# A block's first and last product open and close its sum, and each step puts the products ahead of the query projection

## The reference

```python
def block(xb):
    q = (xb @ w_q).reshape(PEER_BLOCK, PEER_HEADS, 2, PEER_KEY_DIM // 2)
    s1 = jnp.einsum('thd,nd->thn', q[:, :, 0], keys1)
    s2 = jnp.einsum('thd,nd->thn', q[:, :, 1], keys2)
    ...
    gate = jax.nn.softmax(sc, axis=-1)
    act = jax.nn.gelu(jnp.einsum('thkd,td->thk', u_tab[e], xb), approximate=False)
    return jnp.einsum('thk,thkd->td', gate * act, v_tab[e])
```

## Time and profile before

| | before |
|---|---|
| median of 3 runs | 2748.71 us (2748.07 to 2752.73) |
| the profiled execution | 2741.37 us |
| its span in the trace | 2739.6 us |
| PE busy | 2421.6 us (88%) |
| DVE busy | 1590.1 us (58%) |
| ACT busy | 900.0 us (33%) |
| moved by the DMA engines | 935.29 MB, 341 GB/s over the span |
| share of the gathers' queue | 60.8% of 16 engines' span |

### The profile page before, as it was taken

One profiled execution on the slowest core, in us unless ns is written; L12 is line 12 of the kernel. 1 busy time (PEld: TensorE's weight loads), 2 busy tenths in 40 slices (PEclk: granted clock), 3 DMA queues, 4 the chain that ended last, 5 costly groups with the idle time before them and its releaser, 6 DMA issues.

```text
span 2739.6 us, 26850 instructions
## 1 busy us (share of the span) xinstructions
PE 2421.6 (88%) x8530; PEld 1356.4 (50%) x8530; DVE 1590.1 (58%) x3736; ACT 900.0 (33%) x2386; POOL 793.3 (29%) x705
## 2 busy tenths in 40 slices
PE   6999999888998788799898898998998998888786
PEld 3555554356887544455444464443554444334332
DVE  2330012212487775798656798657788557666674
ACT  3100121021122332555424554334644324343332
POOL 0111100000133122343333334334343335444442
PEclk9999999999999889999999999999999999999999
DMA  6222316875898789999999999999999999999996
GB/s 261 100 100 100 115 51 231 328 310 193 314 344 340 280 339 426 406 411 381 426 427 425 425 371 409 426 427 426 413 369 424 423 426 417 427 416 426 426 420 277
DMA packets 143568, 935.29 MB, mean 341 GB/s; under 512 B 16914, under 2 KB 28434, under 8 KB 41026
## 3 DMA queue, kind: packets, MB, share of 16 engines
q0 software_dynamic: 96928, 687.39, 60.8%
q1 hardware_dynamic: 33842, 204.77, 19.1%
q10 hardware_dynamic: 12656, 41.42, 3.8%
HBM read 898.33 MB, written 35.19 MB: 341 GB/s over the span
## 4 chain that ended last, share of the span: by engine, by line
PE 32%; DMA 26%; DVE 12%; ACT 3%; DVEq 2%; issue 2%; POOL 1%; ACTq 1%; POOLq 0%
DMA ring<-in_peer_uv,e_idx 24%; PE e_acc L1803 14%; PE e_acc L1732 5%; DVE ring L1936 5%; PE e_qs L1821 3%; PE e_B L1714 3%; PE e_A L1714 2%; DVEq L1938 2%; DMA e_wb<-in_w_out 1%; POOL ring L1536 1%; ACT e_diag L1652 1%; DMA e_mg<-in_w_late 1%; DVE e_f L1952 1%; PE e_A L948 1%; ACT e_coef L1645 1%
## 5 line engine op out<-in xcount | busy, mean ns | idle before, releaser
L1803 PE MATMUL e_acc<-ring,e_diag 128*128 128x512 f32 x2368 | 1114.8, 618 | 204.7 <-ACT e_diag L1652 204.5
L1536 POOL DMA_INDIRECT ring<-in_peer_uv,e_idx x640 | 753.0, 1177 | 1398.3 <-PE e_acc L1803 1008.8
L1936 DVE CUSTOM_DVE_ANT_0 ring<-ring,e_xb 128x1024 f32<-128x1024 f32 x640 | 774.8, 1224 | 418.9 <-DMA ring<-in_peer_uv,e_idx 397.9
L1803 PEld LDWEIGHTS e_acc<-ring,e_diag 128*128 128x128 f32 x2368 | 448.2, 196 | 785.6 <-issue 481.6
L1642 ACT ACTIVATE e_act<-e_dots 128x2 f32<-128x2 f32 x320 | 65.1, 203 | 734.3 <-DVEq L1938 731.3
L534 PE MATMUL pj<-held,ring 128*128 128x512 f32 x512 | 225.2, 593 | 0.0
L1652 ACT ACTIVATE e_diag<-ident,e_coef 128x128 f32<-128x128 f32 x592 | 206.1, 394 | 20.9
L568 PE MATMUL pj<-ring,held 128*128 128x512 f32 x352 | 156.4, 599 | 10.1 <-DMA ring<-in_w_big 7.9
L1645 ACT ACTIVATE e_coef<-e_act,e_gate 128x1 f32<-128x1 f32 x640 | 153.9, 287 | 23.1 <-issue 1.1
L534 PEld LDWEIGHTS pj<-held,ring 128*128 128x128 f32 x512 | 94.8, 190 | 107.3 <-issue 107.3
L1821 PEld LDWEIGHTS e_qs<-e_h2T,e_w_head 128*128 128x128 f32 x1200 | 141.1, 195 | 10.0 <-issue 9.7
(11 more groups left out here) (405 smaller groups left out, 2338.8 us busy)
## 6 DMA issues: line engine op xcount, KB each, us to landing
e_wb<-in_w_out SPq DMA_DIRECT2D x49, 1024.0 KB, 9.4
ring<-in_w_big SPq DMA_DIRECT2D x18, 2048.0 KB, 9.0
e_w_head<-in_w_q ACTq DMA_DIRECT2D x30, 1024.0 KB, 9.1
ring<-in_w_mod SPq DMA_DIRECT2D x8, 2048.0 KB, 10.3
ring<-in_peer_uv,e_idx POOLq DMA_INDIRECT x640, 12.3
wm<-in_w_mod SPq DMA_DIRECT2D x4, 2048.0 KB, 18.2
e_m<-scratch_mod_rows SPq DMA_DIRECT2D x15, 512.0 KB, 14.7
e_m<-scratch_xbcT SPq DMA_DIRECT2D x7, 1024.0 KB, 14.6
```

What stands on the lines that cost most here:

```text
L1536: nc.gpsimd.indirect_dma_start(expert[:, u % RING, :], None, dr["peer_uv"], bass.IndirectOffsetOnAxis(idx[:, h % 4, s:s + 1], 0)).then_inc ...
L1803: mm = nc.tensor.matmul(acc[:, c * 512:(c + 1) * 512], diag[:, v % RING, :], expert[:, v % RING, D + c * 512:D + (c + 1) * 512], start=Fal ...
L1936: nc.vector.tensor_tensor_reduce(expert[:, u % RING, 0:D], expert[:, u % RING, 0:D], xb[p % 2][:, :], 1.0, 0.0, ALU.mult, ALU.add, dots[:, ...
```

## The change

Three edits. The first product of a block opens the accumulation and the last one closes it, so the 4 matmuls of zeros per block are gone, with the tile of zeros. Who waited for `f_mm` waits for the last product's `slot_free`. And in `body` of PE, `begin` (now only a wait) and `products` stand ahead of the query projection (n = 0) and of the scores (n = 2).

```diff
+FIRST_PRODUCT = [min(u for u in range(SLOTS * p, SLOTS * (p + 1)) if not ON_VECTOR[u]) for p in range(BLOCKS)]
+LAST_PRODUCT = [max(u for u in range(SLOTS * p, SLOTS * (p + 1)) if not ON_VECTOR[u]) for p in range(BLOCKS)]
...
             def block_sum(p):
                 if p:
-                    act.wait_ge(f_mm, p + 1)
+                    act.wait_ge(slot_free, earlier(LAST_PRODUCT[p]) + 1)
...
                     pe.wait_ge(late_free, LATE_UNITS)
-                for c in range(2):
-                    nc.tensor.matmul(acc[:, c * 512:(c + 1) * 512], zero[:, :], z512, start=True, stop=False)
-
-            def end(p):
-                for c in range(2):
-                    last = nc.tensor.matmul(acc[:, c * 512:(c + 1) * 512], zero[:, :], z512, start=False, stop=True)
-                last.then_inc(f_mm, 1)
...
                         mm = nc.tensor.matmul(acc[:, c * 512:(c + 1) * 512], diag[:, v % RING, :],
-                                              expert[:, v % RING, D + c * 512:D + (c + 1) * 512], start=False, stop=False)
+                                              expert[:, v % RING, D + c * 512:D + (c + 1) * 512],
+                                              start=v in FIRST_PRODUCT, stop=v in LAST_PRODUCT)
                     mm.then_inc(slot_free, 1)
...
             def body(m, n):
                 c = m + 2
+                if m >= 0:
+                    if n == 0 and (m == FIRST_ON_PE or m and m % HP == 0):
+                        begin(m // HP)
+                    products(m, n)
                 if c < HEADS:
...
-                if m >= 0:
-                    if n == 0 and (m == FIRST_ON_PE or m and m % HP == 0):
-                        begin(m // HP)
-                    products(m, n)
-                    if m % HP == HP - 1 and n == GROUPS - 1:
-                        end(m // HP)
...
             def first_sum():
-                dve.wait_ge(f_mm, 1)
+                dve.wait_ge(slot_free, earlier(LAST_PRODUCT[0]) + 1)
```

More of the change, by code:

```diff
@@ L1284, in experts @@
         dots, act_v, coef = sb("dots", [P, 2, TOPK]), sb("act", [P, 2]), sb("coef", [P, 4, 2])
-        diag, zero = sb("diag", [P, RING, P]), sb("zero", [P, P])
+        diag, ready = sb("diag", [P, RING, P]), sb("ready", [P, 1])
         ss, root, rr = sb("ss", [P, 1]), sb("root", [P, 1]), sb("rr", [P, 1])
@@ L1322, in experts @@
         dots_ready, diag_ready = sem("dots_ready"), sem("diag_ready")
-        f_mm, acc_free, ss_ready, ms_ready, root_ready, y_ready, y_out, row_in = (
-            sem("f_mm"), sem("acc_free"), sem("ss_ready"), sem("ms_ready"), sem("root_ready"), sem("y_ready"), sem("y_out"),
+        acc_free, ss_ready, ms_ready, root_ready, y_ready, y_out, row_in = (
+            sem("acc_free"), sem("ss_ready"), sem("ms_ready"), sem("root_ready"), sem("y_ready"), sem("y_out"),
             sem("row_in"))
@@ L1696, in _ @@
             ident = t["ident"]
-            z512 = zero[:, :].unsqueeze(1).to_broadcast([P, 4, P])
             def product(p, i):
@@ L2064, in _ @@
             dve_back_init()
-            nc.vector.memset(zero[:, :], 0.0).then_inc(const_ready, 1)
+            nc.vector.memset(ready[:, :], 0.0).then_inc(const_ready, 1)
             interleave(late, back, scan, merge, prepare, body, finish, body_first=True)
```

## The result

| | before | changed kernel |
|---|---|---|
| median, timed side by side (4 runs each) | 2748.79 us (2748.07 to 2752.73) | 2794.37 us (2788.72 to 2798.81) |
| ratio, 95% interval | | 1.0162 [1.0145, 1.0180] |
| span of the profiled execution | 2739.6 us | 2792.8 us |
| PE busy | 2421.6 us | 2444.1 us |
| moved by the DMA engines | 935.29 MB, 341 GB/s | 935.29 MB, 335 GB/s |

The changed kernel is 1.6% slower, some 45 us. The forecast was 2749.8 us with a range up to 2760 us, so it was wrong, and wrong by far more than any of its terms. PE has 40 matmul rows fewer (8490 for 8530) and yet is busy 22.5 us longer.

The account below looks back on a forecast made before the run. The prediction took gathers on the DMA engines as the bound. Its terms, -1.7 - 1.7 + 4.5 = +1.1 us, put the profiled 2741.37 us at 2742.5 and the median 2748.71 at 2749.8 us, range 2741 to 2760 us.

Parts of the forecast that it names:

- What bounds the kernel now: Experts' part: gathers keep DMA full while PE has time to spare; 17.6 us of holes at ends of blocks 0 to 2.
- All other heads: PE's two waits in heads away from the holes: caught up within the head, cost nothing; 2.1 + 3.4 us per head at stake.
- The order at the end of a block: PE's changed list around head 16: 29.5 us to the products of (16, 3), 27.4 before; (16, 0) 7.0 us earlier.
- E: End of PE's products of head 15, step 7, where the 29.5 us sum starts; expected about 1.7 us later.
- its fifth term: Two experts' products on PE (products 1) behind the 2.1 us wait for ACT, at 3.44 us.
- What this does to the gathers: Refill after (16, 3) 1.2 us late per place; taken as 1.5 at three places, 4.5 us, bounds 0 and 10.5.
- the head before: Head 15, also full of scan: waits behind its projection and scores make its end about 1.7 us later.
- rival 1: Waits at three block ends cool PE and hold DVE up: 2755.8 us, up to 2763; chance 0.28.
- The zeros: Pairs of 1.72 us on PE: 1.7 us gained at the end, 1.7 at the first pair; block ends counted elsewhere.
- Rival 2: Holes at block ends close as slots of (16, 0) come free 7 us earlier: 2731 us, half 2740; chance 0.17.
- The signs that were named: Block ends: POOL's first wait 7 us shorter, PE idle 2 and 3.4 us, DVE's L1964 waiting 3 us at three places.
- The two signs that were to prove the prediction wrong: Three places' missing DMA time over 5 us from 17.6 us, or a plain stretch, as at 2580, below 1.0.

Follow-up runs that it names:

- scan_heads_old: The changed kernel with PE's old order of projection, scores and products in heads m % 8 = 6, 7, 0, 1, beside the scan; 2740.97 us, ratio 0.9972.
- first_zeros_gone: The kernel before without the pair of zero matmuls ahead of each block's first product; 2741.13 us, ratio 0.9978.
- last_zeros_gone: The kernel before without the pair of zero matmuls behind each block's last product; 2739.63 us, ratio 0.9975.
- S_copy_behind: The changed kernel with only ACT's copy of S moved behind the run of its step; 2760.51 us, ratio 1.0047.
- zeros_only: The kernel before with all zero matmuls gone and PE's order of projection, scores and products kept; 2737.14 us, ratio 0.9962.
- order_only: The kernel before, zeros kept, with products moved ahead of the projection and the scores on PE; 2809.13 us, ratio 1.0224.
- projection_moved: The changed kernel with products ahead of the projection only, scores ahead of products as before, no zeros; 2758.08 us, ratio 1.0047.

## Why the prediction was wrong, by its own steps

**What bounds the kernel now.** The reading holds: the gathers bound the kernel, and an edit can cost time only by making the DMA engines idle. What failed is the step after it, that the search for such places ended with the windows that already showed a hole. A full window doesn't say how much more PE could take. In head 14 both were full at once: DMA 1.01 and PE 42.75 of 45.4 us. The prediction had such a row in hand, three of its windows showed PE busy for all 20 us, and read from it only where the holes were.

**"All other heads" is the step that failed.** It priced the waits in all heads but the ones at the holes at nothing, since "PE is idle for a fifth of the time" in a plain stretch and "catches up within the head". For the 20 heads m % 8 in 2 to 5 that was nearly true: scan_heads_old has the waits there and is 7.2 us faster than before, and in the changed kernel the heads outside of the scan stretches lose 1.3 us. Of these 20 heads only 5, 13 and 21, right ahead of scan heads, lose something in the changed kernel, by the dot products 1.9, 3.9 and 5.3 us. For the scan heads ahead of a block's last one it was false: heads 6, 14 and 22 lose 21.1 us, in windows that had been full. The price stood in the text as what would be at stake if the cover were gone, "2.1 + 3.4 us per head"; measured in head 14 are waits of 1.99 and 3.29 us and 3.5 us of lower clock, of which 7.1 us came through. The idle share of one stretch at 2580 us had been used for all stretches.

**The order at the end of a block: the walk held, its price did not.** From E to the start of the products of (16, 3) the walk gave 29.5 us; the timeline of the changed kernel, from the row that follows (15, 7), has 1684.81 - 1653.39 = 31.42:

```profile
1653.39 1.04 PE L928 MATMUL e_A<-ident,held 128*128 128x128 f32 x8
...
1667.00 5.40 PE L1799 MATMUL e_acc<-ring,e_diag 128*128 128x512 f32 x8 [1.99 <-ACT e_diag L1656]
...
1684.81 3.61 PE L1799 MATMUL e_acc<-ring,e_diag 128*128 128x512 f32 x4 [3.29 <-ACT e_diag L1656]
```

The 1.9 us over the walk are the products at 1667.00, which took 5.40 us instead of the 3.44 of its fifth term. Both waits came out as worked out, 1.99 for 2.1 and 3.29 for 3.4. What this does to the gathers was taken as 1.5 us per place, 4.5 us. The intervals around the three ends cost 6.3, 5.7 and 5.1 us, 17.1 in all, nearly four times that and more than the upper bound of 10.5 us.

The starts of the products say which part failed. They lag by 28.7 us at (14, 7), 30.4 at (15, 7), 23.3 at (16, 0), 29.0 at (16, 1), 30.4 at (16, 2), 34.3 at (16, 3) and still 34.2 at (17, 7). So the head before did cost its 1.7 us, and (16, 0) did come 7.1 us earlier, as worked out (7.0). (16, 3) comes 5.6 us later than by the lag at (14, 7), for the 3.8 us of the prediction; the 1.9 us between them are the half clock of (16, 1), which the walk left to rival 1. Then the prediction took off most of the delay, since "before, this refill queued", and was left with 1.2 us. Nothing came off: a head later the lag is the same.

**The zeros.** -3.4 us was too small; -9.7 us is measured. The pair at the end was right: in the changed kernel the copy of the sum (L1631) starts at 2781.22, 3.74 us behind the start of the last products at 2777.48. The mis-sized part is the pairs at the ends of blocks 0 to 2, which had been put into the walk and vanished there in a sum with the other sign; by themselves they stand where PE has little time to spare, and first_zeros_gone and last_zeros_gone, 6.3 and 7.8 us faster, fit their being paid in full.

**The rivals.** Rival 1 had the right sign and part of the right mechanism: waits for ACT's diagonals, products at half clock behind them, and DVE's choice later (its wait for the copy of `S` is 63.7 us in 20 places, 18.0 in 4 before), though S_copy_behind has nearly the same waits of DVE, 57.9 us in 19 places, and loses 13 us where the changed kernel loses 46. It too looked only at three places, so its far end was 2763 us, and of the two it put the clock first: in head 14 the waits make 4.9 us of the 8.4 and the clock 3.5. The Trainium skill, "TensorE: Matmul & The Clock Gate", Part 1, says that an idle stretch returns the array to 1.2 GHz. The rows at 1568.02 and 1582.79 agree, the row of zeros_only in the last section, with nearly the same idle time, does not. Rival 2 is refuted: the holes moved and didn't close. POOL's timeline, which answers to the earlier trace rows, shows its waits for the refills of (16, 0), (16, 1) and (16, 3). The first is 5.08 us where it was 11.66, and the others stand behind it:

```profile
1659.99 0.93 POOL L1540 DMA_INDIRECT ring<-in_peer_uv,e_idx  x1 [5.08 <-PE e_acc L1799]
...
1670.14 1.61 POOL L1540 DMA_INDIRECT ring<-in_peer_uv,e_idx  x1 [7.50 <-PE e_acc L1799]
...
1688.69 1.09 POOL L1540 DMA_INDIRECT ring<-in_peer_uv,e_idx  x1 [6.41 <-PE e_acc L1799]
```

**The signs that were named.** PE's two waits, POOL's shorter first wait and the end of the program came as described. DVE's wait for the copy of `S` was to be about 3 us at three places; it came in 20 places, and in head 16 it is 6.80 us:

```profile
1681.97 0.49 DVE L1959 MAX8 e_v<-e_S 128x8 f32<-128x128 f32 x2 [6.80 <-ACT e_S L1681]
```

The two signs that were to prove the prediction wrong, the missing time of the three places and the share of a plain stretch, both stayed in their bounds while the kernel lost 45 us. They tested the places that had been looked at. The share also hid part of what happened at the places themselves, which the bytes show (28.2 against 23.7 us). The sum of bytes over all windows from 1000 us on would have caught both.

## What to carry to other kernels

When an edit makes one engine's in-order list wait for another in every iteration, price it in each kind of iteration apart, in the one where the waiting engine is fullest first, and compare the length of that iteration's list with the length of its transfers; a kernel at 1.01 DMA share can have a second engine at its limit in the same window. If work is put ahead of a matmul whose result another engine copies, try that copy behind the work that the other engine owes in the same step; in its old place the two engines here ran in turns. And two delays can cost more together (55 us here) than the sum of each alone (21 and 14): test them together. A lag between two kernels should be read from an instruction whose place in its list the edit doesn't shift.

## What was unexpected of the hardware

Idle time alone didn't decide PE's clock. In zeros_only, a PE that had waited 1.96 us went on at full rate, and in the changed kernel, at nearly the same place of head 14, one that had waited 1.99 us went on at half rate (the row at 1568.02 above). The row of zeros_only:

```profile
1558.31 3.70 PE L1799 MATMUL e_acc<-ring,e_diag 128*128 128x512 f32 x8 [1.96 <-ACT e_diag L1656]
```

In order_only the same idle time of 2.09 us gave either rate within 8 us, behind the same four rows:

```profile
1557.09 5.40 PE L1803 MATMUL e_acc<-ring,e_diag 128*128 128x512 f32 x8 [2.09 <-ACT e_diag L1652]
1562.32 0.60 PE L1778 MATMUL e_qs<-ident,e_xb 128*128 128x128 f32 x4
1565.01 3.70 PE L1803 MATMUL e_acc<-ring,e_diag 128*128 128x512 f32 x8 [2.09 <-ACT e_diag L1652]
```

What else differs between zeros_only and the changed kernel, where scores and products stood ahead of the one wait and 16 projection matmuls ahead of the other, wasn't tried by itself. In every kernel here that waits behind the projection with nothing in between, that wait was 1.99 us and the products behind it took 5.40 us in head 14 (changed kernel, projection_moved, S_copy_behind, order_only).
